# A Hymba block on one core: adaLN weights loaded in column halves, three projection tiles accumulated in turn, modulation on ScalarE

## The chip, the cores and the metric

The kernel runs on one core of a Trainium2 chip. The metric is the device time of one execution in microseconds (us). The profile's engines are PE (TensorE), PEld (its weight loads), DVE (VectorE), ACT (ScalarE), POOL (GpSimd) and SP (SyncE, which issues all DMAs here).

## What is computed

One layer, batch 1, 1024 tokens, model width 1024, all float32 at the interface:

```python
c_act = silu(c)
mod = c_act @ ada_w + ada_b                      # ada_w: (1024, 3072)
shift, scale, gate = split(mod, 3)
h = rmsnorm(x, norm_g) * (1 + scale) + shift     # (1024, 1024)
z = h @ w_in                                     # (1024, 2760)
xr, gr, q, k, v, ga, qi, ki, wi = split(z)
y_r = rg_lru(conv(xr)) * silu(gr)                # 512 channels in 4 groups of 128
y_a = dsa_attention(q, k, v, qi, ki, wi) * silu(ga)   # 8 heads; an indexer picks the top 256 keys
x = x + gate * (concat(y_r, y_a) @ w_out)
out = rmsnorm(x, final_g)
```

The diff touches what leads from x, c and ada_w to h, and how the first tiles of z are made.

## The kernel before

**The opening.** SyncE issues the eight row blocks of x (512 KB each, L600), then `ada_w[:, 0:2048]`, the shift and scale columns, in eight row blocks of 1 MB (L603), with the weight slabs 0 and 1 behind blocks 6 and 7. ScalarE squares x (L805), GpSimd makes 1/rms (L686, L687), VectorE scales the rows (L1039), TensorE transposes x in groups of four 128x128 tiles (L1335) and ScalarE copies the groups to `xt` (L809). VectorE accumulates c_act times ada_w per row block in `acc`, in two column groups, chunks 0 to 2 and 3 to 7 (`MOD_GROUPS`, L1048, L1051). TensorE sums `acc` over the partitions (L1342), VectorE adds ada_b and norm_g (L1059, L1060) and, chunk by chunk, modulates `xt` (L1061); ScalarE rounds that to fp32r as `h_hi` (L812), and VectorE subtracts for `h_lo` (L1064).

**Projection.** The columns of w_in are cut in tiles of 128 (`TILES`): kiwi (the indexer key and its weights wi, 72 columns), qi 0 to 3, xr and gr in turn four times, gate (from ada_w's last third, no slab), kv, q 0 to 3, ga 0 to 3: 23 tiles, numbered j. A tile has eight steps, one for each chunk k of 128 rows (`kstep`, L1345): six matmuls of 128x512, w_hi h_hi, w_hi h_lo and w_lo h_hi for each half of the tokens (L1373). Tile j accumulates in PSUM pair j % 2, so it waits until tile j-2 has been taken out. The slab of tile w is loaded to `w_raw[w % 2]` (`load_slab`, L590, issued once slab w-2 is split) and GpSimd splits it (`split_slab`, L689): `w_hi` by a rounding pass (L696), `w_lo` in two half-width subtractions (L697, L698), once tile w-2 is projected. Tiles 0 and 1 are partly interleaved, tile 0 chunk by chunk as h comes.

**Behind a tile.** ScalarE takes kiwi, qi, kv, q and ga out of PSUM (`evacuate`, L814), GpSimd makes the low parts (`after_evac`, L710; half_lo is L725, L726), and SyncE moves them into place with DMAs (the "stack" events, L622 to L628). "wi" is eight small transposes (L1390); the first qi tile is taken out after them, since both use `raw`. The indexer has 48 units: a product of qi and key (L1413, L1414), a relu on ScalarE (L875), a weighted sum on VectorE (L1216, L1219). Four recurrence groups follow: convolution on VectorE (L1171, L1175), gates on TensorE (L1422), sigmoids and exponentials on ScalarE (L886 to L905), scan on VectorE (L1226 to L1239). The 256 largest scores are found by a search of 31 bits, counting on ScalarE for three row blocks (L858) and on VectorE for the three others (L1095), with updates on VectorE (L1107, L1109). kv is taken out only when all four groups are through.

**What sets the order.** The function `stages()` (L123) is a planner: each event has an engine, a cost, a rank and what it comes after; a list schedule over these gives a fixed order for each engine (`ORDER`). `FIRST_US` says when each engine is free for it. Indexer products have a lower rank number, that is precedence, over projection steps. Engines then run their order with semaphore waits. The attention behind it (from L1437 on) has an order of its own, by steps g.

## Time and profile before

| | us |
|---|---|
| median of 3 runs | 621.24 (619.52 to 621.46) |
| the profiled execution | 619.93 |
| its span | 618.1 |
| TensorE busy | 535.4 (87%) |
| VectorE busy | 439.5 (71%) |
| ScalarE busy | 377.4 (61%) |
| GpSimd busy | 233.5 (38%) |

The page is of one execution, the profiled one. Busy shares are means over stages with different limits. The span runs from the first to the last instruction of the profile; 1.8 us of the execution's own time lie around it. Times in the rows below are us from the span's start, and a group's mean is in ns.

### The profile page before, as it was taken

Reading aid. Unit: us, or ns where it says so; the run is one execution under the profiler, and the core shown is the slowest. Engines: PE = TensorE matmul, PEld = TensorE weight load, DVE = VectorE, ACT = ScalarE, POOL = GpSimd, SP = SyncE. Lnnn points to the kernel's source line nnn. Section 1 sums busy time; section 2 is a strip of 40 time slices with the busy share of each in tenths; the row PEclk is TensorE's granted clock in tenths of the full one; section 3 lists DMA queues with packets and bytes.
Section 4 is the critical chain, followed back from the end, with each engine's and each line's share of the span. In section 5 each row is a group of like instructions: output and inputs, shape, how many; then the busy total and the mean of one; then the engine's idle time right before and its main releaser. Section 6 shows DMA issues by size and latency. Waiting matters only on the chain.

```text
span 618.1 us, 8029 instructions
## 1 busy us (share of the span) xinstructions
PE 535.4 (87%) x2676; PEld 444.8 (72%) x2676; DVE 439.5 (71%) x992; ACT 377.4 (61%) x679; POOL 233.5 (38%) x195
## 2 busy tenths in 40 slices
PE   1459989998999999999999526489999999999994
PEld 1346868777787777778888415478889999888873
DVE  5987386885999889898697886854475666664522
ACT  6513236453499999987898555554466666656531
POOL 5150862352344274677642003740402030313322
PEclk9859999998999999999999855569999999999999
DMA  8967342430112111135550420110011000101011
GB/s 335 418 206 266 105 118 53 102 85 18 36 34 69 34 36 34 35 103 137 140 133 0 177 96 0 68 36 2 8 61 43 28 36 34 41 30 69 0 69 68
DMA packets 16457, 51.96 MB, mean 84 GB/s; under 512 B 4000, under 2 KB 5024, under 8 KB 15392
## 3 DMA queue, kind: packets, MB, share of 16 engines
q1 hardware_dynamic: 16416, 51.45, 26.3%
q8 instruction: 21, 0.34, 0.2%
q14 instruction: 20, 0.16, 0.1%
HBM read 37.81 MB, written 4.19 MB: 68 GB/s over the span
## 4 chain that ended last, share of the span: by engine, by line
PE 68%; DVE 11%; DMA 7%; POOL 5%; ACT 4%; issue 3%; SPq 2%; DVEq 0%; POOLq 0%; ACTq 0%
PE pair L1373 30%; PE pair L1470 13%; PE pair L1492 6%; PE pair L1505 5%; DMA ada<-in_ada_w 4%; PE pair L1448 3%; PE pair L1449 2%; DMA qs<-half_lo 2%; PE pair L1422 2%; DVE rank L1156 2%; PE pair L1514 2%; PE pair L1413 2%; PE pair L1414 2%; DVE tie L1158 1%; POOL half_lo L726 1%
## 5 line engine op out<-in xcount | busy, mean ns | idle before, releaser
L1373 PE MATMUL pair<-h_hi,w_hi 128*128 128x512 f32 (+1 forms) x352 | 114.4, 407 | 1.6 <-DVE h_lo L1064 1.5
L1373 PE MATMUL pair<-h_lo,w_hi 128*128 128x512 f32 (+1 forms) x352 | 109.8, 393 | 0.0
L1373 PE MATMUL pair<-h_hi,w_lo 128*128 128x512 f32 (+1 forms) x352 | 109.0, 391 | 0.0
L1298 DVE TENSOR_TENSOR pt_lo<-pair,pt_hi 128x512 fp32r<-128x512 f32 (+3 forms) x96 | 50.5, 554 | 71.1 <-ACT pt_hi L963 70.5
L858 ACT ACTIVATE bias_sb<-score_sb,tinies 128x1024 bf16<-128x1024 f32 (+2 forms) x93 | 95.7, 1032 | 3.2 <-DVE tinies L1109 3.1
L696 POOL TENSOR_SCALAR w_hi<-w_raw 128x1024 fp32r<-128x1024 f32 (+1 forms) x22 | 29.4, 1339 | 136.3 <-PE pair L1373 120.5
L1373 PEld LDWEIGHTS pair<-h_hi,w_hi 128*128 128x128 f32 (+1 forms) x352 | 65.0, 188 | 19.0 <-issue 6.2
L1373 PEld LDWEIGHTS pair<-h_lo,w_hi 128*128 128x128 f32 (+1 forms) x352 | 66.0, 188 | 15.5 <-issue 0.8
L1373 PEld LDWEIGHTS pair<-h_hi,w_lo 128*128 128x128 f32 (+1 forms) x352 | 65.6, 186 | 15.4 <-issue 0.7
L1095 DVE TENSOR_SCALAR_CACHE_REDUCE bias_sb<-score_sb,tinies 128x640 bf16<-128x640 f32 (+2 forms) x93 | 72.6, 802 | 0.9
L781 POOL TENSOR_TENSOR x_res<-q_free,x_res 128x512 f32<-128x512 f32 x14 | 18.1, 1296 | 121.0 <-DVE q_free L1269 121.0
L1219 DVE SCALAR_TENSOR_TENSOR score_sb<-relu,tinies,score_sb 128x1024 f32<-128x1024 f32 (+5 forms) x42 | 45.9, 1139 | 18.4 <-ACT relu L875 18.4
L963 ACT ACTIVATE pt_hi<-pair 128x512 fp32r<-128x512 f32 (+3 forms) x96 | 43.5, 488 | 25.3 <-PE pair L1505 22.8
L875 ACT ACTIVATE relu<-pair 128x1024 f32<-128x1024 f32 (+5 forms) x48 | 34.3, 759 | 35.0 <-PE pair L1414 23.5
L1505 PE MATMUL pair<-ident,prob 128*128 128x128 f32 x194 | 31.2, 290 | 20.8 <-ACT prob L971 20.8
L1492 PE MATMUL pair<-pt_hi,v_pair 128*128 128x256 f32 x144 | 39.2, 305 | 6.3 <-DVE o_sb L1312 5.1
L762 POOL TENSOR_TENSOR wo_lo<-wo_raw,wo_hi 128x1024 fp32r<-128x1024 f32 x8 | 20.7, 2597 | 55.8 <-ACT wo_hi L999 55.8
L1505 PEld LDWEIGHTS pair<-ident,prob 128*128 128x128 f32 x194 | 23.7, 147 | 24.5 <-issue 18.1
L1448 PE MATMUL pair<-key_hi,qs 128*128 128x512 f32 (+3 forms) x96 | 40.6, 424 | 0.0
L971 ACT ACTIVATE prob<-prob,tinies 128x256 f32<-128x256 f32 (+7 forms) x43 | 33.4, 776 | 9.4 <-DVE tinies L1255 9.4
L1492 PE MATMUL pair<-pt_lo,v_pair 128*128 128x256 f32 x144 | 37.6, 293 | 0.0
L953 ACT ACTIVATE pv<-pair 128x256 f32<-128x256 f32 x32 | 12.2, 382 | 39.6 <-PE pair L1492 39.5
(195 smaller groups left out, 1254.2 us busy)
## 6 DMA issues: line engine op xcount, KB each, us to landing
w_raw<-in_w_tiles SPq DMA_DIRECT2D x21, 512.0 KB, 3.5
ada<-in_ada_w SPq DMA_DIRECT2D x8, 1024.0 KB, 18.4
x_sb<-in_x SPq DMA_DIRECT2D x8, 512.0 KB, 7.1
ada_g<-in_ada_w SPq DMA_DIRECT2D x8, 512.0 KB, 4.5
qs<-half_hi SPq DMA_DIRECT2D x16, 256.0 KB, 3.6
qs<-half_lo SPq DMA_DIRECT2D x16, 256.0 KB, 4.4
wo_raw<-in_w_out SPq DMA_DIRECT2D x8, 512.0 KB, 6.4
x_res<-in_x SPq DMA_DIRECT2D x8, 512.0 KB, 3.3
```

The lines of the kernel that those rows point to most:

```text
L858: nc.scalar.activation(junk[i], score_sb[:, SCORE_OFF[i]:SCORE_OFF[i] + keys_of(i)], ACT.Sign, bias=cand[:, c:c + 1], scale=-1.0, accum_ou ...
L875: nc.scalar.activation(relu_sb[relus % 2][:, 0:n], pairs[PAIR["idx", o[1]]][:, 0:n], ACT.Relu, scale=HD ** -0.5).then_inc(slot_free, 1)
L963: nc.scalar.activation(pt_hi[:, 4 * b:4 * b + nc4, hh, :], psum[use % 2][:, 0:nc4 * P].rearrange("p (c q) -> p c q", q=P), ACT.Copy).then_ ...
L971: nc.scalar.activation(prob_of(g)[:, 0:n], prob_of(g)[:, 0:n], ACT.Exp, bias=negmax[:, g % 3:g % 3 + 1], scale=-1.0, accum_out=rsum[:, g % ...
L1095: nc.vector.tensor_scalar(junk[PICK[c]], scores(c), cols(c, cand), cols(c, nK), ALU.is_ge, ALU.add, accum_out=cols(c, cnt)).then_inc(count ...
L1219: nc.vector.scalar_tensor_tensor(dst, src, w, dst, ALU.mult, ALU.add).then_inc(summed, 1)
L1298: nc.vector.tensor_tensor(pt_lo[:, 4 * b:4 * b + nc4, hh, :], psum[use % 2][:, 0:nc4 * P].rearrange("p (c q) -> p c q", q=P), f32(pt_hi[:, ...
L1373: ins = nc.tensor.matmul(psum[banks[half]][0:width, :], w[b][:, k, 0:width], hh[:, k, half * HALF:(half + 1) * HALF], start=(k == 0 and p ...
L1448: nc.tensor.matmul(dst, qs[:, h, i * P:(i + 1) * P], key_hi[:, c:c + w], start=True, stop=False)
L1470: ins = nc.tensor.matmul(bank(3), y, w[:, m, half * HALF:(half + 1) * HALF], start=(m == 0 and p == 0), stop=(m == KC - 1 and p == 2))
L1492: ins = nc.tensor.matmul(psum[2][:, 0:256], v_pair[:, c, :], t[:, c, :, :].rearrange("p h q -> p (h q)"), start=(c == 0 and p == 0), stop= ...
L1505: ins = nc.tensor.transpose(psum[use % 2][:, (c % 4) * P:(c % 4 + 1) * P], prob_of(g - LAG_T)[:, c * P:(c + 1) * P], ident[:, :])
```

## The change

- ada_w's shift and scale columns come in two column halves of 512 KB for each row block: chunks 0 to 3 of shift and scale, then 4 to 7. The first halves are loaded in turn with x rows 4 to 7, slab 0 behind half 4; slabs 1 and 2 come before the second halves, slab 3 after the last transpose of x.
- `MOD_GROUPS` is now (0, 4), (4, 8). Each has its own accumulation, sums on TensorE and modulation constants.
- ScalarE modulates: two instructions for a chunk, one to `h_hi` in fp32r, one in place to `xt` in f32, straight from `mod`. VectorE subtracts for `h_lo` on six chunks, GpSimd on chunks 2 and 3.
- Tiles 0, 1 and 2 are accumulated in turn in three PSUM pairs, chunk by chunk (`first_part`, `first_two`, `third`), high parts before low parts. The second sums stand between `third(2)` and `third(3)`.
- `wi` is placed behind all of tile 2 in the planner's constraints, and in PSUM bank 6; the indexer's pairs are swapped, and its second unit waits until tile 2 is taken out.
- Slabs 0 to 3 have buffers of their own (slab 3 over rows 6 and 7 of x); from slab 4 on they go round three buffers. `w_lo` now lies over `w_raw`, so a load waits for the projection of the tile that had the buffer (three tiles earlier) and no longer for a split.
- The planner's free times and costs of the first tiles are changed, so the order may differ anywhere before the attention.

```diff
-MOD_GROUPS = [(0, 3), (3, KC)]
+MOD_GROUPS = [(0, KC // 2), (KC // 2, KC)]
+LO_POOL = (2, 3)
+LO_DVE = [k for k in range(KC) if k not in LO_POOL]
...
+SLAB_BUF = {w: w if w < 4 else (w - 1) % 3 for w in range(NW)}
+SLAB_PREV = {w: max([v for v in range(w) if SLAB_BUF[v] == SLAB_BUF[w]], default=None) for w in range(NW)}
+FIRST = 3
+PROJ_PAIR = {j: j if j < FIRST else (j + 1) % 2 for j in range(NJ)}
...
-FIRST_US = 46.0
+FIRST_US = dict(PE=30.0, ACT=55.0, DVE=56.0, POOL=42.0, SP=40.0)
+FIRST_STEP_US = (3.46, 0.1, 0.6)
...
-    add("PE", ("wi",), 0.9, 1, ("evac", 0), ("kstep", 1, KC - 1))
+    add("PE", ("wi",), 0.9, 1, ("evac", 0), ("kstep", FIRST - 1, KC - 1))
...
+        if u == 1:
+            need.append(("evac", FIRST - 1))
...
@@ SyncE
-                if w >= 2:
-                    sp.wait_ge(w_split, w - 1)
+                if w == FIRST:
+                    sp.wait_ge(xt_ps, 2 * KC)
+                if SLAB_PREV[w] is not None:
+                    sp.wait_ge(proj_done, SLAB_TILE[SLAB_PREV[w]] + 1)
...
+            for t in range(NT // 2):
+                load_x(t)
             for k in range(KC):
+                load_ada(k, 0)
+                if k < NT // 2:
+                    load_x(NT // 2 + k)
+                if k == NT // 2:
+                    load_slab(0)
+            load_slab(1)
+            load_slab(2)
+            for k in range(KC):
+                load_ada(k, 1)
+            load_slab(FIRST)
...
@@ GpSimd
-            split_slab(0)
-            split_slab(1)
+            for w in range(FIRST):
+                split_slab(w)
+            for k in LO_POOL:
+                pool.wait_ge(h_full, k + 1)
+                nc.gpsimd.tensor_tensor(h_lo[:, k, :], xt[:, k, :], f32(h_hi[:, k, :]), ALU.subtract).then_inc(h_lo_pool, 1)
+            split_slab(FIRST)
...
@@ ScalarE
+            def modulate(k):
+                act.wait_ge(mod_ok, k // (KC // 2) + 1)
+                act.wait_ge(xt_act, KC + k + 1)
+                shift, scale = mod[:, k:k + 1], mod[:, 8 + k:9 + k]
+                nc.scalar.activation(h_hi[:, k, :], xt[:, k, :], ACT.Identity, bias=shift, scale=scale).then_inc(h_hi_ok, 1)
+                act.wait_ge(h_hi_ok, k + 1)
+                nc.scalar.activation(xt[:, k, :], xt[:, k, :], ACT.Identity, bias=shift, scale=scale).then_inc(h_full, 1)
+
+            for t in range(NT):
+                square(t)
+                if t >= NT // 2:
+                    copy_xt(2 * (t - NT // 2))
+                    copy_xt(2 * (t - NT // 2) + 1)
+            for u in range(KC, KC + 6):
+                copy_xt(u)
+            modulate(0)
+            copy_xt(KC + 6)
+            copy_xt(KC + 7)
+            for k in range(1, KC):
+                modulate(k)
...
@@ VectorE
+            for k in range(KC):
+                accumulate(k, 0)
+                if k < NT // 2:
+                    normalize(NT // 2 + k)
+            modulation(0)
+            accumulate(0, 1)
+            accumulate(1, 1)
+            low_half(0)
+            accumulate(2, 1)
+            accumulate(3, 1)
+            low_half(1)
+            for k in range(KC // 2, KC):
+                accumulate(k, 1)
+            modulation(1)
+            for k in range(KC // 2, KC):
+                low_half(k)
...
                         if ct:
                             dve.wait_ge(gx_ok, ct)
+                            dve.wait_ge(slot_done, SLOT["gates", ct - 1, 1] + 1)
...
@@ TensorE
+            def first_part(j, k, low):
+                width = TILES[j][2]
+                if k == 0 and not low:
+                    pe.wait_ge(w_split, SLAB[j] + 1)
+                    pe.wait_ge(xt_act, (KC, KC + 6, KC + 8)[j])
+                pe.wait_ge(h_hi_ok, k + 1)
+                if low:
+                    wait_low(pe, k)
...
+            def first_two(k):
+                for low in range(2):
+                    for j in range(2):
+                        first_part(j, k, low)
...
+            for u in range(KC + 6):
+                transpose_x(u)
+            mod_sums(0)
+            for u in range(KC + 6, 2 * KC):
+                transpose_x(u)
+            first_two(0)
+            first_two(1)
+            third(0)
+            first_two(2)
+            third(1)
+            first_two(3)
+            third(2)
+            mod_sums(1)
+            third(3)
+            for k in range(KC // 2, KC):
+                first_two(k)
+            for k in range(KC // 2, KC):
+                third(k)
             for o in ORDER["PE"]:
-                if o[0] == "kstep" and o[1] >= 2:
+                if o[0] == "kstep" and o[1] >= FIRST:
                     kstep(o[1], o[2])
```

## Rows read from the trace of the kernel before

**Rows 1.** The page's slices, tenths busy in 40 slices of 15.45 us.

```profile
PE   1459989998999999999999526489999999999994
...
PEclk9859999998999999999999855569999999999999
```

**Rows 2.** The chain of waits in order of time: start, us, what.

```profile
92.40 1.42 PE pair L1373 x6
95.07 1.38 PE pair L1373 x6
...
270.94 65.52 PE pair L1373 x288
```

**Rows 3.** The timeline: start us, us, engine, line, what, [idle before].

```profile
37.42 2.10 POOL L696 TENSOR_SCALAR w_hi<-w_raw 128x1024 fp32r<-128x1024 f32 x1 [0.15 <-DMA w_raw<-in_w_tiles]
...
70.92 0.66 PE L1390 MATMUL pair<-ident,raw 8*128 8x8 f32 x8
...
73.86 2.28 POOL L725 TENSOR_TENSOR half_lo<-raw,half_hi 128x512 fp32r<-128x512 f32 x1
...
85.22 0.47 PE L1413 MATMUL pair<-key_hi,qs 128*128 128x512 f32 x1 [2.52 <-DMA qs<-half_lo]
...
87.53 1.29 POOL L725 TENSOR_TENSOR half_lo<-raw,half_hi 128x512 fp32r<-128x512 f32 x1
```

**Rows 4.** Busy time by stretch, us and instructions of each engine, clock, DMA.

```profile
85.20:163.00 77.80, 73.94 (x331) 60.42 (x332) 56.72 (x53) 39.75 (x54) 26.65 (x18) 0.98 0.27 68
163.00:347.30 184.30, 183.10 (x782) 145.32 (x781) 160.94 (x493) 160.69 (x244) 96.97 (x75) 1.00 0.24 64
```

**Rows 5.** The timeline at the end of the projections.

```profile
346.71 0.62 PE L1373 MATMUL pair<-h_hi,w_lo 128*128 128x512 f32 x2
...
347.36 1.02 ACT L841 ACTIVATE ga<-pair 128x1024 f32<-128x1024 f32 x1 [1.75 <-PE pair L1373]
```

**Rows 6.** ScalarE's waits from 163 to 250 and from 250 to 341.

```profile
ACT L886 <- PE pair L1422: 3.9, 2, 3.0
...
ACT ga L841 <- PE pair L1373: 4.2, 2, 2.6
ACT raw L847 <- PE pair L1373: 3.4, 1, 3.4
```

**Rows 7.** The timeline of the opening.

```profile
1.17 3.83 SPq L600 DMA_DIRECT2D x_sb<-in_x  x8
...
35.53 3.08 DVE L1051 SCALAR_TENSOR_TENSOR acc<-ada,tinies,acc 128x768 f32<-128x768 f32 x2 [1.14 <-DMA ada<-in_ada_w]
...
36.67 6.99 PE L1342 MATMUL pair<-tinies,acc 128*128 128x1 f32 x32 [14.54 <-DVE acc L1051]
...
40.92 2.44 DVE L1061 TENSOR_SCALAR xt<-xt,tinies 128x1024 f32<-128x1024 f32 x2
...
45.14 1.10 PE L1373 MATMUL pair<-h_hi,w_hi 128*72 128x512 f32 x2 [1.49 <-DVE h_lo L1064]
...
49.43 0.63 PE L1373 MATMUL pair<-h_hi,w_lo 128*72 128x512 f32 x2
```

**Rows 8.** Instructions by form until 62 us: count, busy, mean ns, idle before.

```profile
L1051 DVE SCALAR_TENSOR_TENSOR acc<-ada,tinies,acc 128x1280 f32<-128x1280 f32 x7 | 11.3, 1621 | 0.0
...
L1064 DVE TENSOR_TENSOR h_lo<-xt,h_hi 128x1024 fp32r<-128x1024 f32 x7 | 8.5, 1219 | 0.4 <-ACT h_hi L812 0.4
...
L812 ACT ACTIVATE h_hi<-xt 128x1024 fp32r<-128x1024 f32 x8 | 8.4, 1058 | 24.8 <-DVE xt L1061 24.8
```

**Rows 9.** Busy time by stretch again; the last number is GB/s moved.

```profile
4.00:12.00 8.00, 0.00 (x0) 0.00 (x0) 4.95 (x19) 5.88 (x11) 3.49 (x9) 1.00 1.01 390
...
24.00:30.00 6.00, 0.00 (x0) 0.00 (x0) 5.98 (x6) 0.00 (x0) 0.00 (x0) 0.63 1.01 421
...
348.00:352.00 4.00, 0.00 (x0) 0.00 (x0) 3.89 (x9) 0.39 (x1) 0.00 (x0) 0.72 0.86 318
```

**Rows 10.** The page's DMA issues: KB each, median us to landing.

```profile
w_raw<-in_w_tiles SPq DMA_DIRECT2D x21, 512.0 KB, 3.5
```

More of the change, by code:

```diff
@@ L583, in f32, with wait_low, slab_use @@
             return ap.bitcast(F32)
+        def wait_low(engine, k):
+            if k in LO_POOL:
+                engine.wait_ge(h_lo_pool, LO_POOL.index(k) + 1)
+            else:
+                engine.wait_ge(h_lo_ok, LO_DVE.index(k) + 1)
+        def slab_use(w):
+            return sum(SLAB_BUF[v] == SLAB_BUF[w] for v in range(w + 1))
         block = ctx.enter_context(nc.Block())
@@ L1343, in _ @@
                 ins.then_inc(mod_ps, 1)
+            def first_part(j, k, low):
[6 more added lines that the diff above has]
+                    wait_low(pe, k)
+                w_high, w_low = w_hi[SLAB_BUF[SLAB[j]]], w_lo[SLAB_BUF[SLAB[j]]]
+                for p, (w, hh) in enumerate([(w_high, h_lo)] if low else [(w_high, h_hi), (w_low, h_hi)]):
+                    for half in range(2):
+                        ins = nc.tensor.matmul(psum[proj_ps[PROJ_PAIR[j]][half]][0:width, :], w[:, k, 0:width], hh[:, k, half * HALF:(half + 1) * HALF],
+                                               start=(k == 0 and p == 0 and low == 0), stop=(k == KC - 1 and low == 1))
+                if k == KC - 1 and low:
+                    ins.then_inc(proj_done, 1)
             def kstep(j, k):
                 kind, n, width = TILES[j]
-                banks = proj_ps[j % 2]
+                banks = proj_ps[PROJ_PAIR[j]]
                 if k == 0:
```

193 lines of the change are left out of this document (96 added, 97 removed).

## The prediction, made before the changed kernel was run

> **What bounds the kernel now.** I read the page's slices first [rows 1]. TensorE is busy at nine tenths or more from slice 3 to slice 22, that is from 45 us to about 347 us, and its granted clock is full there but for the opening and the stretch behind 348 us. So before 348 us TensorE is the first suspect. The chain of waits agrees: it holds an unbroken run of 288 projection matmuls in 65.52 us [rows 2], 0.2275 us each. Tile 2 is over at 82.7 and TensorE idles 2.5 us until the first indexer product at 85.2 [rows 3]. The table by stretch [rows 4] has the two stages behind it: the indexer stage to 163, and from 163 to 347.3, where TensorE is busy for 183.1 of 184.3 us. VectorE and ScalarE have 160.9 and 160.7 us of work in that same stretch, so both are near it and neither is idle for long. The end of the stretch [rows 5] shows who is last: the last projection matmuls run to 347.2, and only then can ScalarE take the last ga tile, for which it had waited 1.75 us. Three of ScalarE's waits for TensorE in that stretch [rows 6] are 3.9 + 4.2 + 3.4 = 11.5 us. So an earlier TensorE lets ScalarE move up. Behind 348 us comes the attention, whose steps the diff leaves alone; I carry it over unchanged, 270 us.
>
> **The opening, as it stands** [rows 7]. Loads are issued from 1.2 us. The last ada_w row block is accumulated from 35.53, right as it lands. x (4.19 MB), eight ada_w blocks (8.39) and the kiwi slab (0.29) are 12.9 MB in 34.3 us, 375 GB/s with all latency in it. Then TensorE sums over partitions (32 instructions in 6.99 us, 0.22 each), VectorE modulates the first chunk from 40.92, which is 1.6 us behind the 12 sums of the first group, and the first projection matmul starts at 45.14 at half clock (1.10 us for an overlapping pair; 0.63 from 49.43, at full clock). The work of tiles 0, 1 and 2 plus the wi transposes is over at 82.7.
>
> **Part 1: ada_w in halves, x between.** Before shift and scale of chunks 0 to 3 are known, only x, the kiwi slab and the first halves must land: 4.19 + 0.29 + 4.19 = 8.7 MB, at 375 GB/s 23.1 us, so 24.3 instead of 35.5. Slabs 1 and 2 are in at 27.1 (9.7 MB), the last second half at 38.3 (13.9 MB). VectorE's instruction on 1024 columns I take as 1024/1280 of 1.62 = 1.30 us [rows 8]. First group: 24.3 + 1.3 + 16 sums x 0.22 (3.5) + 1.6 to the modulation gives 30.7 us. What the sum rests on is the rate. In the windows [rows 9], with x rows of 512 KB in the queue 390 GB/s are moved, with the 1 MB blocks 421; the later w_out loads, also 512 KB, 318 in their first 4 us. No row has 2 KB runs in numbers, so 318 and 421 are my bounds; 375 is kept, being over the same kind of queue. At 318 the first half lands at 28.5 and the second at 45; at 421 they land at 21.8 and 34.3.
>
> The Trainium skill (DMA: Bandwidth & Descriptors, Rules for kernel authors) asks for at least 1 MiB in one DMA for full bandwidth, which speaks against pieces of 512 KB. The trace has 390 against 421 GB/s, so queued pieces pay little. With the page's fixed 2.0 us on each of 16 pieces not overlapped, the second half would come over 20 us later (an estimate from the page), and the gain would be gone.
>
> **Part 2: modulation on ScalarE.** A chunk takes two ScalarE instructions of 1.06 [rows 8], 2.2 us with the hand-over, in place of three instructions in turn on VectorE, ScalarE and VectorE. VectorE keeps six subtractions of 1.22, GpSimd gets two (2.6 us each by its half-width instructions of 1.29 [rows 3]). TensorE wants a chunk of two tiles in 12 matmuls, 2.7 us, and with the third tile 4.1; so ScalarE's 2.2 keeps ahead. First h_hi at 30.7 + 1.06, about 31.7, where TensorE starts, 13.4 us earlier than 45.1.
>
> GpSimd must split slabs 0, 1, 2 (up to 4.7 us each, 2.10 + 2 x 1.29 [rows 3]) before its two subtractions: done 35, 38 to 40, 43. TensorE needs slab 2 at 40 and these chunks at 42 and 45: covered, by 2 us at least. That cover thins where both work in SBUF: a half subtraction takes 2.28 us beside VectorE's accumulations and 1.29 alone [rows 3]. The Trainium skill (SBUF — State Buffer) says that the two engines hold a shared port pair exclusively; by that rule all of GpSimd's chain stretches, up to 3 us on TensorE, inside my range.
>
> **Part 3: three tiles in turn.** From 31.7 to about 36.5 at half clock: 12 matmuls in 5.2 us (0.43 each). Then 132 at 0.2275 are 30.0 us; the second group of sums stands in the middle (16 at 0.11 to 0.22: 1.8 to 3.5, take 2.2); the wait for the first chunk of the second half behind it 0.3 and for its low part 0.5. Sum: 31.7 + 5.2 + 30.0 + 2.2 + 0.8 = 69.9. With a warm clock and the 421 GB/s (start 28, no slow stretch) it is 64. I take 68, nearer the slow end since the slow clock has a row. With wi 0.6 the same work that ended at 82.7 ends at 68.6: a lead of 14.1 us.
>
> **Part 4: slab buffers.** Slabs 0 to 3 need no earlier tile, so the 2.5 us gap before the first indexer product gets filled by tile 3: lead 16.6. From slab 4 on, w_lo overwrites w_raw, so a load waits until tile w-3 is projected: 3.5 us of landing [rows 10] and 4.7 us of split against two tiles of 10.9 us (48 x 0.2275); hidden with 13 us to spare. In return no split waits for TensorE ahead of half_lo on GpSimd.
>
> **Part 5: what follows.** The indexer stage hangs on wi, which now stands behind all of tile 2: at 68.0 instead of 70.92. From wi to the first product 14.3 us pass [rows 3] (half_hi and raw, GpSimd 4.5, the stack transfers); nothing there changes. So this stage starts only 2.9 us earlier, while TensorE has 13.7 us more of projection behind it. In it TensorE is busy 73.9 of 77.8 us [rows 4], filling one projection step (six matmuls) in every 2.7 us between indexer products [rows 2]; I let the new order do the same, less 2 us of idle that came from late tiles. After it, 163 to 347.3, TensorE has ten steps less. Could ScalarE and VectorE follow? They have 160.7 and 160.9 us of work and would be given 184.3 - 16.6 + 2.9 + 2 = 172.6. It fits, at 93%, which costs some new waiting; the search counts fill gaps. Of 16.6 us of lead I give back 2.6 for that. Small edits go with it: the convolution's new wait for the earlier gates was over before anyway (0), the first indexer unit in pair 2 waits for tile 2's evacuation, which ScalarE does ahead of its relu in either kernel (0 to 1 us), the six further DMA issues lie beside transfers (0).
>
> **Forecast.** 14 us gained. The profiled execution took 619.93 us (span 618.1), 1.3 under the median of the runs, 621.24; against its own time 606, against the median 607. I say 606.5.
>
> **Rivals.**
> - ScalarE and VectorE become the bound: TensorE's lead is then an idle engine, and only the 2.9 us of the indexer's earlier start, 2 us of its idle and a few of the 11.5 us of waits are gained. For: 160.9 of 184.3 busy; against: the waits for TensorE are real gaps. 7 us, 613. Chance 0.18.
> - The lead is larger: warm clock, 421 GB/s, tile 2 ends at 64, and nothing is given back: 20 us, 600. For: TensorE has transposes and sums right before. Chance 0.13.
> - The halves come slowly (318 GB/s, or the port takes its 3 us): first half 4 us, second 7 us later, tile 2 ends at 74: 8 us, 612. Chance 0.07.
> - Slower than before: SyncE's queue runs in order, and a slab load that waits for tile w-3 stands before the transfers of a qi stack. In the indexer stage a tile takes 8 x 2.7 = 21.5 us, so one such wait can hold the stack, and VectorE and ScalarE with it, 21.5 us. Beyond a hold of 14 us it decides: 606.5 + 21.5 = 628, 7 over the median. Against: load 7, the first that waits for a qi tile, waits for the last one, whose stack can't come earlier. Chance 0.06.
> - The change does not do what it says: transfers land together rather than in order, so the first halves are no earlier. Against: the blocks were consumed one by one in order. 620. Chance 0.03.
> - Forecast: 0.53.
>
> What the measurement of this kernel can tell from no change is about 0.3%, 1.9 us. Faster by more: 0.53 + 0.18 + 0.13 + 0.07 = 0.91; within 0.03; slower 0.06. The range goes from below the larger-lead case to above the ones at 612 and 613: 598 to 616.
>
> **What would show it.** Right: first projection matmul at 28 to 34; wi at 64 to 71; first indexer product 14 us behind it; no idle before it on TensorE; last projection matmul at 331 to 337, a span of 602 to 606. The steps wrong: VectorE waiting for ada_w beyond 30 us (rate); TensorE gaps between 36 and 60 (GpSimd or the low parts late); TensorE idle between 163 and 330 while ScalarE's and VectorE's busy shares pass 95% (work-bound). The forecast falls if the last projection matmul ends well before the search does, or if stack transfers follow a long blocked load on SyncE's queue.

## The result, and the profile after

The changed kernel takes 639.1 us (median of 4 runs, 635.7 to 639.2) against 621.1 for the kernel before (4 runs, 619.5 to 621.5). The ratio is 1.028, with a 95% interval from 1.024 to 1.032. It is slower by 18 us, where 606.5 was forecast and 598 to 616 given as the range.

The profiled execution took 639.2 us (span 637.3). The page's slices, of 15.9 us each:

```profile
PE   2499986999999998999999106478999999999994
...
PEclk9879998999999999989999755559999999999998
```

TensorE is at nine tenths from about 32 us, one slice earlier than before [rows 1]. The two slices with 1 and 0, from about 350 to 382 us, are the news. They show in the timeline of TensorE, ScalarE and VectorE, ahead of the attention (start us, us, engine, line, what, idle before and who ended it):

```profile
94.03 0.67 PE L1547 MATMUL pair<-key_hi,qs 128*128 128x512 f32 x1 [2.47 <-DMA qs<-half_lo]
108.53 0.80 PE L1547 MATMUL pair<-key_hi,qs 128*128 128x512 f32 x1 [5.83 <-ACT relu L950]
...
351.94 1.03 ACT L916 ACTIVATE ga<-pair 128x1024 f32<-128x1024 f32 x1 [1.76 <-PE pair L1482]
...
364.74 1.34 DVE L1233 TENSOR_SCALAR_CACHE_REDUCE bias_sb<-score_sb,tinies 128x1024 bf16<-128x1024 f32 x1
...
384.07 0.66 PE L1639 MATMUL pair<-ident,prob 128*128 128x128 f32 x2 [31.70 <-ACT prob L1046]
```

The last two rows in the kernel before, which I had not read when I predicted:

```profile
348.13 1.34 DVE L1140 TENSOR_SCALAR_CACHE_REDUCE bias_sb<-score_sb,tinies 128x1024 bf16<-128x1024 f32 x1
...
365.76 0.66 PE L1505 MATMUL pair<-ident,prob 128*128 128x128 f32 x2 [17.97 <-ACT prob L971]
```

TensorE idled 18 us ahead of the attention in the kernel before already, for the first row of probabilities, which comes out of the search. From that matmul to the end it is 252.3 us before and 253.2 after, and between 251.7 and 253.9 in every run below. So the time is decided at the first prob. Six dates of each traced execution, in us from its start (gates: the first gates matmul; ga: ScalarE takes the last projection tile; settled: VectorE begins to check the thresholds that ScalarE's counts have found, the DVE rows above):

| kernel | wi | first indexer product | gates | ga | settled | first prob | median time |
|---|---|---|---|---|---|---|---|
| before | 70.9 | 85.2 | 161.8 | 347.4 | 348.1 | 365.8 | 621.1 |
| changed | 75.7 | 94.0 | 177.3 | 351.9 | 364.7 | 384.1 | 639.1 |

The loss of 16.6 us at "settled" can be added up by way of ga: the first indexer product comes 8.8 later, the indexer stage is 83.3 us long instead of 76.6 (6.7), from gates to the last ga TensorE needs 174.6 instead of 185.6 (11.0 gained: eleven projection steps fewer, 66 of its matmuls, which are 15.0 us at 0.2275), and ScalarE's part of the search is over 12.8 us behind ga instead of 0.7 (12.1 lost).

Without ga the sum is simpler, and says more. Gates come 15.5 us later, and from gates to settled it takes 187.5 us instead of 186.3. So that stage is as long as before: TensorE's eleven steps fewer gave it nothing, and the loss lies ahead of it, in the opening and the indexer stage. Another 1.7 us go between settled and first prob: in VectorE's planned order three of its own counts stand behind settled, where one stood before.

**The opening** in TensorE's timeline:

```profile
29.89 3.58 PE L1438 MATMUL pair<-tinies,acc 128*128 128x1 f32 x16 [2.75 <-DVE acc L1127]
...
35.98 1.10 PE L1453 MATMUL pair<-h_hi,w_hi 128*72 128x512 f32 x2 [0.71 <-ACT h_hi L872]
...
53.34 1.84 PE L1438 MATMUL pair<-tinies,acc 128*128 128x1 f32 x16
...
75.70 0.66 PE L1522 MATMUL pair<-ident,raw 8*128 8x8 f32 x8
```

The first projection matmul is 9.2 us earlier than before [rows 7], and wi is 4.8 us later [rows 3], since it stands behind three tiles. **GpSimd behind it:**

```profile
75.36 1.28 POOL L747 TENSOR_TENSOR w_lo<-w_raw,w_hi 128x512 fp32r<-128x512 f32 x1
77.19 1.13 POOL L745 TENSOR_SCALAR w_hi<-w_raw 128x1024 fp32r<-128x1024 f32 x1 [0.55 <-DMA w_raw<-in_w_tiles]
78.40 2.13 POOL L746 TENSOR_TENSOR w_lo<-w_raw,w_hi 128x512 fp32r<-128x512 f32 x1
80.50 2.27 POOL L747 TENSOR_TENSOR w_lo<-w_raw,w_hi 128x512 fp32r<-128x512 f32 x1
82.74 2.27 POOL L778 TENSOR_TENSOR half_lo<-raw,half_hi 128x512 fp32r<-128x512 f32 x1
```

ScalarE had tile 1 in raw at 78.5; the split of slab 5 stands ahead of half_lo and even waits for its load. In the kernel before the split there was over when raw was ready, and half_lo began at once [rows 3]. **ScalarE in the indexer stage:**

```profile
96.01 1.51 ACT L950 ACTIVATE relu<-pair 128x1024 f32<-128x1024 f32 x2
105.73 1.02 ACT L921 ACTIVATE half_hi<-pair 128x1024 fp32r<-128x1024 f32 x1 [8.21 <-DMA qs<-half_lo]
```

The evacuation of tile 3 stands behind relu 1 (behind relu 13 before) and waits 8.2 us for the stack transfers of tile 2 to read half_hi; all relus wait behind it. TensorE's clock adds to that: the stage's 329 instructions of TensorE take 76.0 us instead of 72.7, at a granted clock of 0.94 instead of 0.98. That is 3.3 of the 6.7 us. **ScalarE in the late stage** (from gates on), its waits from 177.3 to 365 (line, who ended the wait, us, times, longest):

```profile
ACT raw L922 <- issue: 7.7, 3, 3.9
ACT rnn_a L961 <- PE pair L1556: 6.3, 4, 2.2
ACT ga L916 <- PE pair L1482: 6.2, 3, 2.7
```

and what it does when TensorE's last tile is gone (one line of the code: its form, count, first and last start):

```profile
L933 ACT ACTIVATE bias_sb<-score_sb,tinies x9: 921/1029/1138, 352.9 to 361.2; 128x1024 bf16<-128x1024 f32 x3, 128x896 bf16<-128x896 f32 x3, 128x768 bf16<-128x768 f32 x3
```

ScalarE is early at six of the seven evacuations of tiles 16 to 22, waits 7.7 + 6.2 = 13.9 us there, and has nine counts of the search left at the end. For `raw` the profile names no releaser ("issue"); I read it as TensorE, which run 7 names for the same wait. The order written by the planner has 8 or fewer counts ahead of each evacuation from tile 15 on, and 9 behind the last, where the kernel before has none. The waits themselves are not new: at the same tiles the kernel before has 6.0 + 3.4 + 2.8 = 12.2 us. Its order does 30 counts ahead of the gate tile, that of the changed kernel 21; these are the nine.

### The profile page after: what moved, and what is told of

The parts are those of the page before. It is cut to its first block, busy times and chain, and to the rows that moved or that the text cites. A ratio compares the mean times of both kernels' runs of the same rounds, so it can differ in the third digit from the quotient of the medians.

```text
span 637.3 us, 8079 instructions
## 1 busy us (share of the span) xinstructions
PE 541.0 (85%) x2676; PEld 448.0 (70%) x2676; DVE 440.4 (69%) x982; ACT 387.3 (61%) x686; POOL 243.2 (38%) x197
## 4 chain that ended last, share of the span: by engine, by line
PE 61%; DVE 16%; ACT 7%; issue 6%; DMA 5%; POOL 2%; SPq 2%; DVEq 0%; POOLq 0%; ACTq 0%
PE pair L1482 22%; PE pair L1604 13%; PE pair L1626 5%; PE pair L1639 5%; PE pair L1453 3%; PE pair L1582 2%; PE pair L1583 2%; DMA x_sb<-in_x 2%; PE pair L1556 2%; DVE score_sb L1313 2%; DVE rank L1249 2%; PE pair L1648 2%; DVE acc L1127 2%; DMA qs<-half_lo 2%; PE pair L1547 1%
## 5 line engine op out<-in xcount | busy, mean ns | idle before, releaser
L1482 PE MATMUL pair<-h_hi,w_hi 128*128 128x512 f32 x304 | 99.4, 409 | 1.8 <-ACT rnn_gr L969 1.8
L1482 PE MATMUL pair<-h_lo,w_hi 128*128 128x512 f32 x304 | 94.8, 393 | 0.0
L1482 PE MATMUL pair<-h_hi,w_lo 128*128 128x512 f32 x304 | 94.8, 393 | 0.0
L1482 PEld LDWEIGHTS pair<-h_hi,w_hi 128*128 128x128 f32 x304 | 57.3, 192 | 16.5 <-issue 6.4
L1482 PEld LDWEIGHTS pair<-h_lo,w_hi 128*128 128x128 f32 x304 | 57.8, 190 | 12.6
L1482 PEld LDWEIGHTS pair<-h_hi,w_lo 128*128 128x128 f32 x304 | 57.6, 190 | 12.5
L745 POOL TENSOR_SCALAR w_hi<-w_raw 128x1024 fp32r<-128x1024 f32 (+1 forms) x22 | 26.8, 1219 | 57.4 <-DMA w_raw<-in_w_tiles 57.4
L1547 PE MATMUL pair<-key_hi,qs 128*128 128x512 f32 (+1 forms) x80 | 30.4, 383 | 9.7 <-ACT relu L950 7.1
```

The source lines that it names most:

```text
L1482: ins = nc.tensor.matmul(psum[banks[half]][0:width, :], w[b][:, k, 0:width], hh[:, k, half * HALF:(half + 1) * HALF], start=(k == 0 and p ...
L1547: nc.tensor.matmul(dst, qs[:, h, i * P:(i + 1) * P], key_hi[:, c:c + w], start=True, stop=False)
```

## The experiments

All are edits of the changed kernel unless said otherwise; ratios are against the kernel before, with their 95% intervals. `place` moves one step of an engine's planned order behind another.

**1. Halves of tile 1 ahead of split 5**

```diff
+place("POOL", ("after", 1), ("split", 4))
```

> One edit to the changed kernel: GpSimd takes the halves of tile 1 (half_lo) ahead of the split of slab 5 instead of behind it. Theory A (the loss lies in the orders behind the opening, and every us of the indexer stage's end reaches the end of the kernel): in the trace of the changed kernel half_lo was ready to start at 78.5 and started at 82.7, so the first indexer product comes at about 89.7 instead of 94.0, the late stage keeps its 187 us, and the time falls by about 4 us, 639 to 635. Rival B (the indexer stage is bound elsewhere, by TensorE's slabs or by the waits for stack transfers, which have their own dates): the first product comes earlier, but gates(0,0) stays within 1 us of 177.4 and the time within 1 us of 639. Rival C (split 5 is needed early): TensorE idles for the split of slab 5, and the time rises.

637.4 us, ratio 1.028 (1.027 to 1.030). No theory's number: first product at 93.1, not 89.7, gates at 176.6. half_lo now came at once, at 80.3, but wi itself came 1.7 us later in this trace, the transfers landed at 90.7, and TensorE had four steps of tile 4 ahead of the first product in its own order. One edit uncovers the next queue.

**2. Tiles 3 and 4 evacuated later**

```diff
+place("ACT", ("evac", 3), ("relu", 7))
+place("ACT", ("evac", 4), ("relu", 21))
```

> One edit to the changed kernel: ScalarE evacuates tile 3 behind relu 7 and tile 4 behind relu 21, instead of behind relu 1 and relu 7. Theory A: the wait of 8.2 us for the stack transfer of tile 2 ahead of relu 2, the 5.8 us that TensorE idles behind it and the half clock from 108.5 to 115 go; the indexer stage shrinks from 84 to 76-78 us, the late stage keeps 187 us, the time falls by 6 to 8 us, 639 to 632. Rival B: another wait takes its place (relu 8 waits as long, or tile 5's projection, which waits for that evacuation, is late), the stage stays over 82 us and the time over 637.

636.1 us, ratio 1.025 (1.022 to 1.028). Between A's and B's number. The wait of 8.2 us is gone, the stage is 81.0 us instead of 83.3. As rival B had it, another wait took part of its place: TensorE's tile 5, next in its order behind the eighth product, now waits 3.1 us for tile 3's evacuation, and tile 6 waits 3.0.

**3. Both, and wi inside tile 2**

```diff
             for k in range(KC // 2, KC):
                 third(k)
+                if k == KC - 3:
+                    transpose_wi()
```

> Both edits of order, and wi computed by TensorE in the middle of tile 2's projection, as soon as the kiwi tile is evacuated, instead of behind tile 2. Theory A: wi at about 71.5 instead of 75.7, first indexer product at about 85.5, gates(0,0) at about 162 to 164, as in the kernel before; the late stage again 186 to 187 us, so the time is 621 to 625: the loss against the kernel before is gone and nothing is gained, although TensorE has 10 to 14 us less to do behind the indexer stage. Rival D (TensorE's lead is worth something once the indexer stage is on time): the late stage shrinks to 175-180 and the time is 610 to 615. Rival B: the parts do not add up, the time stays over 632.

634.2 us, ratio 1.022 (1.020 to 1.025), B's number. wi at 72.0, first product at 91.8, gates at 171.8: still 6.6 and 10 us behind the kernel before, for the four steps of tile 4 and the two waits named above.

**4. Splits behind the accumulations**

```diff
+            pool.wait_ge(acc_ok[0], KC)
             for w in range(FIRST):
                 split_slab(w)
```

> One edit to the changed kernel: GpSimd begins its slab splits only when VectorE has accumulated the eighth first half. In the changed kernel VectorE's last four accumulations of the first half took 1.78 us each beside the splits, the three before them 1.28. If the two engines hinder each other in SBUF (theory P; the Trainium skill, SBUF - State Buffer, has a port pair that they hold in turns): these four take about 1.3 each, the first sums start 1.8 to 2 us earlier, at 28; GpSimd's own halves take 1.27 instead of 1.64 to 2.1, the splits of slabs 0 to 2 end within 3 us of 35.7, and the first projection matmul comes 0 to 2 us earlier than 35.98. If the long ones are due to landing data (theory L), they still take 1.78 and the first sums stay at 29.9. In either case the time moves by under 2.5 us.

639.1 us, ratio 1.030 (1.028 to 1.032). VectorE in the first group, changed kernel, then this one:

```profile
22.69 7.14 DVE L1127 SCALAR_TENSOR_TENSOR acc<-ada,tinies,acc 128x1024 f32<-128x1024 f32 x4
```

```profile
23.76 5.45 DVE L1128 SCALAR_TENSOR_TENSOR acc<-ada,tinies,acc 128x1024 f32<-128x1024 f32 x4
...
43.94 10.97 DVE L1128 SCALAR_TENSOR_TENSOR acc<-ada,tinies,acc 128x1024 f32<-128x1024 f32 x4
```

The four take 1.36 us each with GpSimd idle and 1.79 beside it: theory P. The first projection matmul comes at 33.0 instead of 36.0. But the splits now meet the second group (2.74 us each), and TensorE waits for slab 1 (1.6 us until 36.5); wi is at 77.4. It only moves the trouble.

**5. Replanned opening**

```diff
-FIRST_US = dict(PE=30.0, ACT=55.0, DVE=56.0, POOL=42.0, SP=40.0)
-FIRST_STEP_US = (3.46, 0.1, 0.6)
+FIRST_US = dict(PE=36.0, ACT=65.4, DVE=66.6, POOL=55.0, SP=40.0)
+FIRST_STEP_US = (4.05, 0.05, 0.68)
-SPLIT_US = 3.9
+SPLIT_US = 4.7
+LAND_US = 4.0
...
-                need.append(("stack", stacks[stacks.index(j) - 1]))
+                need.append((("stack", stacks[stacks.index(j) - 1]), LAND_US))
...
-        need = [(("stack", J["qi", h // 2]), 2.8), (("stack", J["kiwi", 0]), 2.8), ("wi_out",)]
+        need = [(("stack", J["qi", h // 2]), LAND_US), (("stack", J["kiwi", 0]), LAND_US), ("wi_out",)]
```

> wi in the middle of tile 2 as in the third run, and the four orders planned again: the planner gets the times at which the opening really ends (TensorE's first step 36.0, ScalarE free at 65.4, VectorE 66.6), and a stack transfer counts as landed 4.0 us behind its issue (3.7 us from the last issue to the release in the traces), for the indexer and for the next evacuation alike. It now puts the halves of tile 1 ahead of split 5, evacuates tile 3 behind relu 7 and tile 4 behind relu 15, and gives TensorE two steps of tile 4, not four, before the first indexer product. Theory A: in the third run those four steps held the first product to 91.8 although the transfer had landed at 89.5; so it comes at 89.5 or before, the stage takes 78 us or less, gates(0,0) at 167 or before, the late stage keeps its 187 us, the time is 624 to 629. Rival B (the waits only change places): stage 80 us or more, time as in the third run, 632 to 635. Rival D (TensorE's lead is worth something in the late stage): under 620.

(wi is placed as in 3.) 629.4 us, ratio 1.015 (1.011 to 1.018). The indexer stage is 76.9 us, as before the change, and gates come at 168.6 (expected 167). The changed kernel's planner had TensorE, ScalarE, VectorE and GpSimd free 6 to 13 us too early, and counted a stack as landed at once for the next evacuation and 2.8 us behind its issue for the products. Behind gates nothing changed: 186.7 us to settled.

**6. No GpSimd beside the accumulations**

```diff
-LO_POOL = (2, 3)
+LO_POOL = ()
...
+            pool.wait_ge(acc_ok[1], KC)
             split_slab(FIRST)
...
-            for k in range(KC // 2, KC):
-                accumulate(k, 1)
+            accumulate(4, 1)
+            low_half(2)
+            accumulate(5, 1)
+            accumulate(6, 1)
+            low_half(3)
+            accumulate(7, 1)
```

> The changed kernel with all eight low halves on VectorE (1.22 us each) and none on GpSimd (3.2 us each there), the third and fourth of them between the accumulations of the second half, and the split of slab 3 only behind the last accumulation; the orders are unchanged. In the changed kernel the four last accumulations of the second half took 2.49 us each beside GpSimd's low halves, against 1.28 to 1.36 with GpSimd idle. Theory P (the two engines hinder each other in SBUF): VectorE does the eight accumulations and four low halves in about 15.5 us, the second sums start at 50 instead of 53.3, tile 2 ends at about 71 instead of 74.2, wi comes 3 us earlier; with the orders as they are, the time falls by 1 to 3 us. Theory L (the accumulations were slow because of the transfers that land meanwhile): they still take 2.4 to 2.5, the two more low halves come on top, second sums at 55, time 639 or more.

634.2 us, ratio 1.023 (1.021 to 1.024). The last accumulations of the second group and the sums behind them:

```profile
44.67 2.67 DVE L1128 SCALAR_TENSOR_TENSOR acc<-ada,tinies,acc 128x1024 f32<-128x1024 f32 x2
...
48.39 1.28 DVE L1128 SCALAR_TENSOR_TENSOR acc<-ada,tinies,acc 128x1024 f32<-128x1024 f32 x1
...
53.15 1.84 PE L1443 MATMUL pair<-tinies,acc 128*128 128x1 f32 x16
```

They fall from 2.49 us each to between 1.28 and 1.34 and are over at 49.7 instead of 52.5. wi did not move (75.5), because the second sums stand behind TensorE's own steps and begin at 53.2 all the same. So the mechanism holds and its price on the path to wi was nil. The time fell by 4.9 us even so: in the traces the first product comes 1.4 us earlier (92.6), which gates keep, 2.4 are gained from gates to the first prob and 1.3 in the attention. What made these is not shown; they are of the size that the last section gives for differences between executions, but they add up one way.

**7. Tile 16 projected twice**

```diff
+                if j == 16 and k == KC - 1 and not again:
+                    for kk in range(KC):
+                        kstep(j, kk, True)
+                elif k == STEPS[j] - 1:
```

> The changed kernel with tile 16 projected twice (48 more matmuls, 10.9 us of TensorE's work in the late stage; the result of the second pass is used). Theory A (the late stage is 187 us of ScalarE's and VectorE's work, and TensorE's lead of 12 us there is idle time): the last projection matmul moves from 352 to about 360 to 362, the time stays within 2 us of 639. Rival D (TensorE still bounds part of the late stage, the gain went elsewhere): the time rises by 5 to 11 us.

648.1 us, ratio 1.046 (1.044 to 1.049): 9.0 us more. My theory that TensorE's lead lay idle fell with this, or so it seemed: ScalarE waits for the tile with its counts behind it.

```profile
295.81 1.03 ACT L922 ACTIVATE raw<-pair 128x1024 f32<-128x1024 f32 x1 [10.28 <-PE pair L1482]
```

**8. The search prepared earlier**

```diff
+place("DVE", ("prep",), ("nonneg", 5))
```

> The changed kernel with VectorE's preparation of the search ahead of the convolution of channel tile 1 instead of behind it, as in the kernel before. Theory A says nothing of it. Theory S (part of the late stage's 187 us is a later start of the search: 186 counts of ScalarE follow the signs in order): ScalarE's and VectorE's counts begin about 5 us earlier, and the time falls by 2 to 5 us. Theory W (total work bounds, not its start): the first count is earlier but gates(1,0) later, and the time stays within 1.5 us of 639.

641.1 us, ratio 1.034 (1.031 to 1.036), 2 us more. This does not test theory S, since the counts did not begin earlier: ScalarE's first is 18.7 us behind gates with and without the edit (197.5 and 196.0 in the traces). In the kernel before it is 18.9, so ScalarE's part of the search did not start late in the changed kernel. VectorE's own counts do, 15.8 us behind gates instead of 12.2, and 17.7 with the edit; what that costs was not tested.

**9. Nine counts moved on ScalarE**

```diff
+SEGMENTS = dict(zip((16, 17, 18, 19, 20, 21, 22), (8, 10, 9, 8, 8, 8, 8)))
+order = ORDER["ACT"]
+start = order.index(("evac", 15)) + 1
+counts = [o for o in order[start:] if o[0] == "count_a"]
+rest = [o for o in order[start:] if o[0] == "cmp"]
+del order[start:]
+for j, n in SEGMENTS.items():
+    order += counts[:n] + [("evac", j)]
+    del counts[:n]
+order += counts + rest
```

> The changed kernel with one edit, in ScalarE's order: of the nine counts of the search that stand behind the evacuation of tile 22, two are put ahead of the evacuation of tile 16, four ahead of 17, one ahead of 18 and two ahead of 20. Since the run with tile 16 projected twice cost 9 us, theory A's second half (TensorE's lead in the late stage is idle time) has fallen. Theory O (order): in the changed kernel ScalarE is at each of these evacuations before TensorE has the tile, and idles there 14 us in all (2.3, 3.9, 1.5, 2.8, 1.7, 1.8 us), and does nine counts of about 1.03 us when TensorE has ended at 352. So the waits shrink to under 6 us, the last projection stays at 352, the search is over at 355 to 357 instead of 364.7, and the time falls by 7 to 9 us, 639 to 631. Theory W (the stage is as long as ScalarE's and VectorE's work): the waits move to the counts, which then wait for VectorE, and the time stays within 2 us of 639.

627.8 us, ratio 1.011 (1.009 to 1.014): 11.3 us less (7 to 9 expected), from one engine's order. ga at 352.4 as before the edit, settled at 353.2 instead of 364.7, and at the evacuations:

```profile
299.80 1.01 ACT L935 ACTIVATE raw<-pair 128x1024 f32<-128x1024 f32 x1
310.18 1.03 ACT L935 ACTIVATE raw<-pair 128x1024 f32<-128x1024 f32 x1
321.56 1.03 ACT L929 ACTIVATE ga<-pair 128x1024 f32<-128x1024 f32 x1
330.80 1.01 ACT L929 ACTIVATE ga<-pair 128x1024 f32<-128x1024 f32 x1
341.53 1.03 ACT L929 ACTIVATE ga<-pair 128x1024 f32<-128x1024 f32 x1 [1.51 <-PE pair L1495]
352.41 1.02 ACT L929 ACTIVATE ga<-pair 128x1024 f32<-128x1024 f32 x1 [1.76 <-PE pair L1495]
```

Theory W falls.

**10. The planner's costs of the search**

```diff
-COUNT_A_US = (1.38, 1.27, 1.16)
-COUNT_US = (0.98, 0.84, 0.71)
-OWN_US = 0.45
-UPDATE_US = 0.48
-UPDATE_LAG = 0.8
+COUNT_A_US = (1.15, 1.04, 0.94)
+COUNT_US = (0.88, 0.75, 0.61)
+OWN_US = 0.36
+UPDATE_US = 0.38
+UPDATE_LAG = 0.5
```

> The changed kernel with one edit in the planner: the costs of the search's steps as the trace has them. A count on ScalarE 1.15, 1.04, 0.94 us instead of 1.38, 1.27, 1.16; on VectorE 0.88, 0.75, 0.61 instead of 0.98, 0.84, 0.71; the small steps 0.36 to 0.5 instead of 0.45 to 0.8. It now plans 4 counts instead of 9 behind the evacuation of tile 22, and 9 or 10 between two evacuations instead of 8. Theory O: it does by itself most of what the run before does by hand, the time falls by 6 to 10 us, to 629-633. Theory W: within 2 us of 639.

624.7 us, ratio 1.008 (1.006 to 1.009): 14.4 us less, above my range. The planner took a count for a fifth to a quarter longer than it is (1.38 us for 1.13 from start to start, at 1024 columns), so it gave ScalarE too few between two tiles. The new order has none behind tile 22, and from gates to settled it takes 172.5 us instead of 187.5.

**11. All together** (5 with its wi, 6 and 10 in one kernel; the planner has ScalarE and VectorE free 3 us earlier than in 5, at 62.4 and 63.6)

> The changed kernel with all of it: wi in the middle of tile 2, the orders planned with the real end of the opening and the landing of the stacks, no GpSimd work beside VectorE's accumulations, the search's costs as the trace has them. If the parts add up (A for the indexer stage, O for the late one): wi at about 69.5, first indexer product at 87 to 89, gates(0,0) at 164 to 166, a late stage of 176 to 180 us, time 611 to 618, faster than the kernel before by 2 to 9 us. If theory W holds the late stage stays at 187 and the time is 624 to 627.

610.6 us, ratio 0.985 (0.983 to 0.987). Faster than the kernel before by 9.2 us, in runs side by side, and than the changed kernel by 28.5. The parts add up (9.7 + 4.9 + 14.4 = 29.0).

**12. The kernel before, with edit 10 alone**

> The kernel before, with the search's costs in its planner as the trace has them and nothing else. Its TensorE is busy to 347.2 and has no lead; theory O says that a better order of counts and evacuations is worth little there: TensorE's last projection stays at 347 within 1 us, the search is over before it, by up to 10 us, and the time falls by 0 to 3 us, 620 to 618. Theory W: no change (within 1 us). If it falls by over 5 us, the search and not TensorE set the end of that stage in the kernel before, against my reading of its trace.

605.7 us, ratio 0.977 (0.975 to 0.979): 14.2 us less, where I gave 0 to 3. By the condition I had written down, the search and not TensorE set the end of that stage in the kernel before. From gates to settled it takes 172.4 us, as in run 10 (172.5): the wrong costs took the same 14 us from either kernel, and with the right ones the change still costs 19.0 us (624.7 against 605.7). TensorE's last tile is even later (ga at 350.4, not 347.4), yet:

```profile
353.87 0.66 PE L1505 MATMUL pair<-ident,prob 128*128 128x128 f32 x2 [3.03 <-ACT prob L971]
```

**13. Two more edits of the opening's order on 11**

```diff
             first_two(3)
+            mod_sums(1)
             third(2)
-            mod_sums(1)
             third(3)
...
+place("POOL", ("after", 1), ("after", 0))
```

> The kernel with all edits together (610.6 us) with two more: TensorE takes the second group of sums ahead of tile 2's third step instead of behind it, since VectorE had the accumulations ready at 49.8 and the sums began at 53.3, TensorE being busy; and GpSimd takes tile 1's halves ahead of split 4, since they were ready at 74.9 and began at 77.8. Theory A: kiwi tile 2 us earlier, half_lo 2.9 us less behind it, first indexer product at 84 to 86 instead of 89.0, and as the indexer stage and the search behind it keep their length, the time falls by 3 to 5 us, to 605.5-607.5. Theory W2 (VectorE's work in the search is by now the bound and its start does not matter): the time stays at 609 to 611.

610.1 us, ratio 0.984 (0.982 to 0.986): no change. The transfers landed 3.2 us earlier (85.8), but the first product came at 88.4, TensorE's steps of tiles 3 and 4 being ahead of it, and gates at 166.2. The kiwi tile came 0.5 us earlier, not 2. This is no proof of W2, since the start of the stage hardly moved.

**14. Tile 16 twice, on 11**

> The kernel with all edits together, with tile 16 projected twice (10.9 us more for TensorE); the same edit cost 9 us in the changed kernel. In the kernel with all edits TensorE ends its projections at 337.6 and then idles 17.2 us for the first prob of the attention, and ScalarE waits for TensorE only 8 us behind the gates. Theory O: with the order repaired the lead is real slack, the added work costs under 4 us (611 to 614). If it costs 8 to 11 us again (theory D: TensorE's pace sets the end of the search through the evacuations in any order), TensorE still bounds that stage, and the idle 17 us are no slack.

620.0 us, ratio 0.9995 (0.9985 to 1.0005): 9.4 us more again, against theory O as I had put it. Yet TensorE still idles ahead of the attention, with 10.9 us more work done:

```profile
365.19 0.66 PE L1652 MATMUL pair<-ident,prob 128*128 128x128 f32 x2 [15.35 <-ACT prob L1048]
```

**15. The same, and the planner told of it**

```diff
-FIRST_STEP_US[j] if j < FIRST else 1.37
+FIRST_STEP_US[j] if j < FIRST else (2.74 if j == 16 else 1.37)
```

> As the run before (all edits together, tile 16 projected twice), but the planner is told that the steps of tile 16 take twice as long. TensorE's work is the same; ScalarE's order now has 15 counts of the search, not 9, ahead of the evacuation of tile 16, and none behind tile 22. Theory O (the 9 us came from ScalarE standing at tile 16 with its counts behind it, and TensorE's 17 us of idle ahead of the attention are slack that a fitting order can use): the search is over at about 335-338 again and the time is 610 to 614, against 620.0 without the planner's knowledge. Theory D (TensorE's pace bounds the search's end in any order): 618 to 621.

608.7 us, ratio 0.9805 (0.9782 to 0.9827). TensorE does the same 10.9 us of added work as in 14, its last tile comes at 351.0, and the time is 11.2 us less than there and no longer than without the added work (610.6):

```profile
355.60 0.66 PE L1652 MATMUL pair<-ident,prob 128*128 128x128 f32 x2 [4.14 <-ACT prob L1048]
```

Theory D falls: TensorE's lead in this kernel was slack. What cost 9.4 us in 14 was a fixed order that put ScalarE in front of a tile that was not there. Run 7, where ScalarE stood the same way for 10.3 us, is read by it; the changed kernel was not planned again for that work.

The dates of the runs that decide:

| kernel | wi | first indexer product | gates | ga | settled | first prob | median time |
|---|---|---|---|---|---|---|---|
| 5 replanned | 74.1 | 91.7 | 168.6 | 345.5 | 355.4 | 375.4 | 629.4 |
| 9 nine counts | 77.3 | 94.4 | 177.7 | 352.4 | 353.2 | 372.5 | 627.8 |
| 11 together | 71.6 | 89.0 | 165.7 | 338.4 | 336.0 | 356.0 | 610.6 |
| 12 before, counts | 71.2 | 85.4 | 164.2 | 350.4 | 336.5 | 353.9 | 605.7 |
| 14 twice | 71.6 | 89.1 | 166.0 | 349.4 | 345.1 | 365.2 | 620.0 |
| 15 twice, planned | 73.0 | 90.5 | 167.4 | 351.0 | 334.8 | 355.6 | 608.7 |

From gates in run 11, for 185 us, VectorE is busy for 172.2 us (columns as in [rows 4]):

```profile
165.70:350.70 185.00, 171.55 (x727) 134.75 (x725) 172.23 (x521) 164.36 (x255) 89.72 (x69) 0.98 0.30 86
```

## Why the prediction was wrong

Two steps failed. The forecast had the stage behind the indexer shrink with TensorE's work, from 184.3 to 172.6 us, and the indexer stage start 2.9 us earlier. In the traces the first gives nothing (187.5 us from gates to settled, 186.3 before), and the indexer stage starts 8.8 us later and takes 6.7 us more.

- **"So before 348 us TensorE is the first suspect", and the attention "carried over unchanged, 270 us".** This is the step on which the whole gain hung. I read that TensorE was never idle and ended last [rows 4, 5], and did not ask what started the next stage. It was the search, with TensorE idle 18 us ahead of the first prob; runs 9, 12 and 15 show it, the last two with TensorE later and the time shorter. The busy share told of an engine that is full, not of one that is waited for. The attention itself was carried over rightly: what went wrong is the date from which it runs.
- **Part 5, "Could ScalarE and VectorE follow? ... It fits, at 93%".** As work it does fit: in run 9 the last tile keeps its date, and the search is over 0.8 us behind it. It failed as order. The engines run a list made ahead, with counts costed 20% too long, and in the changed kernel nine of them stand behind the last tile, so the search ends 12.8 us behind it: all of the lead is gone, where I gave back 2.6. The wrong costs alone are not the cause, since the kernel before had them too; with them either kernel's stage takes 186 to 188 us, and without them either takes 172 (runs 10 and 12), with eleven steps of TensorE fewer or not. The steps fewer are eleven, not ten: by 82.7 us the kernel before has done 150 matmuls, which is tiles 0 to 2 and a step of tile 3, so the lead that I counted was 1.4 us too large.
- **Part 3, tile 2 over at 68.** It ended at 74.2. The three tiles took the 38.2 us of my sum (69.9 - 31.7); what was off is their start, 4.3 us late, and the 1.9 us by which I had rounded the sum down. The first sums began at 29.9 where I had 25.6 (24.3 + 1.3), and ScalarE's first modulation at 34.6 instead of 30.7. The last x row was normalized only at 22.0, and the accumulations behind it took 1.79 us, not 1.30. In the second group they took 2.49 beside GpSimd. I had the cause and put "up to 3 us on TensorE" beside it, as a cost of GpSimd's; it was paid in VectorE's time. By the Trainium skill (SBUF — State Buffer, Who interferes with whom) a VectorE instruction with two SBUF inputs contends with a GpSimd instruction that reads SBUF. Runs 4 and 6 agree (1.36 and 1.28 to 1.34 us with GpSimd idle). Run 6 shows also that it was not on the path to wi in the second group, where TensorE's own steps were.
- **Part 1, the rate.** Right. From 12 to 30 us the pieces of 512 KB moved at 386 GB/s (row below), against 390 and 421 before [rows 9], and VectorE waited for no half. The Trainium skill (DMA: Bandwidth & Descriptors, Rules for kernel authors) wants 1 MiB or more in a DMA for full bandwidth; by this trace pieces of half that cost little in a queue. The page's 2.0 us, which it measured on DMAs issued from GpSimd, did not show on these, which SyncE issues.

```profile
12.00:30.00 18.00, 9.79 (x57) 9.35 (x57) 13.99 (x12) 11.79 (x22) 10.18 (x13) 0.89 1.06 386
```

- **Part 2.** Right: ScalarE's two instructions took 1.24 us each, not 1.06, and kept ahead (TensorE waited once for h_hi among the tiles, 0.2 us); the first projection matmul at 36.0 was outside 28 to 34 by the late sums alone.
- **Part 4, "In return no split waits for TensorE ahead of half_lo".** Wrong in effect. No split waited for TensorE, but loads now do, and in the planned order split 5, behind such a load, stood ahead of half_lo: 4.3 us.
- **Part 5, "From wi to the first product 14.3 us pass ... nothing there changes".** It took 18.3 us, for that split. wi itself was 4.8 us late. Together the 8.8 us.
- **"I let the new order do the same".** It did not: the evacuation of tile 3 moved from relu 13 to relu 1, and the stage is 6.7 us longer. Moving it and tile 4's back behind later relus wins 2.3 (run 2); the replanned orders of run 5 win all but 0.3.
- **The rivals.** My slower rival (a slab load that blocks SyncE's queue ahead of a stack, up to 21.5 us, 628) had the sign and named the wrong queue: SyncE held no stack. The queues that held were GpSimd's, ScalarE's and TensorE's own. "ScalarE and VectorE become the bound", 613, was nearest in kind: its words that "TensorE's lead is then an idle engine" came true, its 2.9 us of earlier start did not.

The forecast's own test caught it: it "falls if the last projection matmul ends well before the search does". It ended 12.8 us before.

What stays open: why run 12 beats run 11 by 5 us. Their traces, 2.3 us apart, show where: ScalarE's part of the search is over at about the same date (settled at 336.5 and 336.0), but in run 11 VectorE has four of its own counts behind that date, in run 12 one, and the mask waits for them. The instruction behind VectorE's last count, in run 12 and in run 11:

```profile
341.60 0.16 DVE L1123 SCALAR_TENSOR_TENSOR tinies<-tinies 128x3 f32<-128x3 f32 x1
```

```profile
343.75 0.16 DVE L1222 SCALAR_TENSOR_TENSOR tinies<-tinies 128x3 f32<-128x3 f32 x1
```

From the first indexer product to it are 256.2 us in run 12 and 254.7 in run 11, and the first product is 3.6 us later in run 11 (89.0 against 85.4). So the late opening may well be the loss. That much is argued: an opening with wi ahead of tile 2's work was not tried, and the rest of the 5 us shows in no trace.

## What to carry to other kernels

An engine busy to the end of a stage need not be what the next stage waits for: look at the first instruction behind the stage and at who ended its wait. Where an order is planned ahead, a change of one stage re-deals every queue; read the new order, engine by engine, for steps that stand in front of something late, and set the planner's costs from the trace before judging the change. In this case five constants were worth 14 us in either kernel, and the change that was made cost 18 us with the wrong ones and 19 with the right ones.

## What the runs showed of the hardware that was not expected

The same pause of TensorE may or may not cost clock. Ahead of the transposes at line 1529 (1538 in run 1) both traces have one of 1.59 us. Changed kernel, then run 1:

```profile
273.17 0.71 PE L1529 MATMUL pair<-ident,raw 64*128 64x64 f32 x8 [1.59 <-ACT raw L914]
...
276.37 1.05 PE L1482 MATMUL pair<-h_lo,w_hi 128*128 128x512 f32 x2
```

```profile
271.50 0.71 PE L1538 MATMUL pair<-ident,raw 64*128 64x64 f32 x8 [1.59 <-ACT raw L923]
...
276.35 0.62 PE L1491 MATMUL pair<-h_hi,w_hi 128*128 128x512 f32 x2
```

In the one, pairs of matmuls take 1.05 us from 275.5 to 278, the lower level of 1.2 GHz, and the granted clock from 274 to 286 is 0.86 (46 matmuls). In the other they stay at 0.62, at 2.4 GHz, and the clock at 1.00 (55 matmuls). That is about 2 us, and the runs of the changed kernel spread over 3.6. So differences of under 2 us between single traces of such kernels, as in run 1, are not to be read.

And beside GpSimd's subtractions one accumulation of VectorE on 1024 columns went from 1.28 us to as much as 2.7, more than twice its time.
